# The latent attention sections of a two-block transformer: where filler work stands between the jobs

## The reference

```python
h = x * (1.0 + scale[:, None]) + shift[:, None]
hc = cx * (1.0 + scale_c) + shift_c
(a_q, a_i, a_ff, a_fb, b_q, b_k, b_v, c_q, c_k, c_v, d_q, d_k, d_v, g_lat) = jnp.split(h @ w_in, SPLIT_AT, axis=-1)
... # the same fourteen parts of hc @ w_in for the context
y_a, yc_a = hgrn2_mixer(a_q, a_i, a_ff, a_fb, a_qc, ..., ctx_out)       # gated linear recurrence
y_b = merge_heads(global_gqa(qB, [kB, kBc], [vB, vBc]))                 # attention over latent and context keys
y_c = merge_heads(diff_attention(qC, [kC, kCc], [vC, vCc], lam, ...))   # differential attention
y_d = merge_heads(window_gqa_latent(qD, kD, vD, kDc, vDc, wn_sink))     # window attention
y = jnp.concatenate([y_a, y_b, y_c, y_d], axis=-1) * jax.nn.silu(g_lat)
x_new = layer_norm(alpha * x + gate[:, None] * (y @ w_out), ln_g, ln_b)
```

## Time and profile before

| | |
|---|---|
| median of 3 executions | 1631.5 us |
| profiled execution | 1634.02 us, span 1631.9 us |
| PE busy | 1477.5 us (91%) |
| DVE, ACT, POOL busy | 544.0, 476.0, 146.0 us |
| section two0, from its attention's first logits to its layer norm's end | about 992 to 1323 us |
| section two1 | about 1323 to 1632 us |

### The profile page before, as it was taken

The page is one execution under the profiler, slowest core; times in us unless marked ns, Lnnn a source line. Parts: engine busy times, 40 slices in busy tenths (PEclk is TensorE's granted clock), DMA queues, the critical chain, the costliest instruction groups (busy, mean ns, idle before and its releaser), DMA issues. The chain is left out here.

```text
span 1631.9 us, 20313 instructions
## 1 busy us (share of the span) xinstructions
PE 1477.5 (91%) x8186; PEld 1194.2 (73%) x8186; DVE 544.0 (33%) x1273; ACT 476.0 (29%) x791; POOL 146.0 (9%) x191
## 2 busy tenths in 40 slices
PE   5999999999899999999999999988977866788874
PEld 3887887888788788888888886766765755566654
DVE  1352122112153223233453213556343113563321
ACT  2122333110212333341322424233453014334322
POOL 0111100000010200001110000222000001330000
PEclk8999999999999999999999999998987978898977
DMA  8544344554354444443333343522421312111100
GB/s 360 212 173 163 137 178 155 184 203 181 137 203 177 155 157 177 152 149 129 117 118 128 110 149 147 214 104 104 155 72 70 129 52 103 52 52 52 52 1 26
DMA packets 30765, 219.87 MB, mean 135 GB/s; under 512 B 3792, under 2 KB 3920, under 8 KB 4304
## 3 DMA queue, kind: packets, MB, share of 16 engines
q1 hardware_dynamic: 30672, 218.57, 36.4%
HBM read 217.51 MB, written 1.05 MB: 134 GB/s over the span
## 5 line engine op out<-in xcount | busy, mean ns | idle before, releaser
L811 PE MATMUL event<-u,ring 128*128 128x256 f32 x3200 | 728.6, 388 | 24.2 <-DVE u L1606 13.2
L811 PEld LDWEIGHTS event<-u,ring 128*128 128x128 f32 x3200 | 616.3, 194 | 128.8 <-issue 43.1
L804 PE MATMUL event<-ring,u 128*128 128x256 f32 (+1 forms) x704 | 153.2, 377 | 0.0
L804 PEld LDWEIGHTS event<-ring,u 128*128 128x128 f32 x704 | 130.4, 194 | 22.2 <-issue 5.4
L985 PE MATMUL event<-region,ring 128*128 128x256 f32 x544 | 119.1, 379 | 2.9 <-DVE region L1626 2.9
L1153 ACT ACTIVATE region<-event 128x512 f32<-128x512 f32 x72 | 43.0, 597 | 255.0 <-PE event L811 254.6
L985 PEld LDWEIGHTS event<-region,ring 128*128 128x128 f32 x544 | 102.8, 190 | 17.9 <-issue 4.2
L896 PE MATMUL logits<-region 64*128 64x256 f32 (+4 forms) x320 | 68.5, 531 | 49.4 <-ACT PT L1198 32.3
L1812 POOL TENSOR_TENSOR raw<-raw,tables 128x512 f32<-128x512 f32 (+1 forms) x28 | 34.0, 1215 | 862.5 <-DVE turned L1469 546.2
L1182 ACT ACTIVATE S<-logits,stat 128x512 f32<-128x512 f32 (+2 forms) x160 | 83.9, 536 | 88.9 <-DVE stat L1504 82.4
L960 PE MATMUL event<-region,ring 128*128 128x256 f32 x384 | 84.4, 380 | 0.0
(11 more groups left out here) (200 smaller groups left out, 1315.8 us busy)
## 6 DMA issues: line engine op xcount, KB each, us to landing
ring<-in_w SPq DMA_DIRECT2D x202, 1024.0 KB, 4.8
tables<-in_two SPq DMA_DIRECT2D x1, 1600.0 KB, 9.5
x<-in_x SPq DMA_DIRECT2D x1, 1024.0 KB, 15.5
x<-in_ctx SPq DMA_DIRECT2D x1, 1024.0 KB, 6.6
out<-x SPq DMA_DIRECT2D x1, 1024.0 KB, 3.9
tables<-in_one SPq DMA_DIRECT2D x1, 832.0 KB, 8.5
tables<-in_late SPq DMA_DIRECT2D x1, 512.0 KB, 5.7
consts<-in_common SPq DMA_DIRECT2D x1, 320.0 KB, 3.2
```

Of the source, the lines that this page charges most:

```text
L804: ins = mm(bank[:, t * 256:t * 256 + width], mem.u[:, q, k, t * P:(t + 1) * P], wt[:, k * 256:k * 256 + width], start=k == 0, stop=k == KB ...
L811: ins = mm(bank[:, j * 256:(j + 1) * 256], wt[:, k * 256 + j * P:k * 256 + j * P + P], mem.u[:, q, k, :], start=k == 0, stop=k == KB - 1)
```

## The change

Three edits. First, the wait quoted above stays only where one of jobs n-2, n-1, n is of kind C (stick-breaking attention of the first block, which uses the tile `turns` for logits too). Second, the filler of `two0` is laid out anew: from about one and a half blocks per job in the first half to one block per job through to job 14; the modulation groups are spread likewise, and the context's `kk` and `vv` leave the attention. Third, the context's `vv`, `fv` and `kk` stand at the end of `two0`, between and behind `mean` and `var` (the context's `fk` stays behind the last job). With `kk` so late, `sq gk1` and `norm gk1`, the norm of the context's keys, go from `two0` to the start of `two1`, and the first logits there wait for it.

```diff
--- before.py
+++ after.py
@@ -260,29 +260,28 @@
-    for h, items in ((0, [proj("hq")]), (1, [proj("hi")]), (2, [proj("nq")]), (3, [("rot", "nq", 0)]), (4, [out(1)]), (5, [out(2)]),
-                     (6, [out(3)]), (7, [("mean", 1)]), (8, [proj("fk"), ("var", 1)]), (9, [proj("fq"), ("rot", "fk", 0)]),
-                     (10, [proj("fv"), ("rot", "fq", 0)]), (11, [("mod", "v1"), ("feed", 1, "v1")]),
...
-                     (26, [proj("vv", 1)]), (28, [("gate", 0, 0)])):
+    for h, items in ((0, [proj("hq")]), (2, [proj("nq")]), (3, [("rot", "nq", 0)]), (4, [out(1)]), (6, [proj("hi")]), (7, [out(2)]),
+                     (9, [proj("fk")]), (10, [out(3)]), (11, [("mean", 1), ("rot", "fk", 0)]), (12, [proj("fq"), ("var", 1)]),
+                     (13, [("rot", "fq", 0)]), (14, [proj("fv"), ("mod", "v1"), ("feed", 1, "v1")]), (15, [proj("ff", 1)]),
...
-    for h, items in ((18, [("decay", 1)]), (19, [("prep", 1, "khat")]), (21, [("khatT", 1)]), (23, [("state", 1)])):
+    for h, items in ((20, [("decay", 1)]), (22, [("prep", 1, "khat")]), (24, [("khatT", 1)]), (26, [("state", 1)])):
         fill[h] += items
-    for g, h in enumerate((1, 3, 5, 7, 13, 16)):
+    for g, h in enumerate((1, 5, 8, 11, 16, 20)):
         fill[h] += group("v1", g)
         fill[h + 1].append(("ada", g, "v1"))
     s += weave(len(jobs), fill)
     s += [("sq", "f0"), proj("fk", 1), ("norm", "f0"), ("gate", 0, 1)] + [("out", i, (0,)) for i in range(4)]
-    return s + [proj("fv", 1), ("mean", 0), ("var", 0), ("feed", 0, "v1")]
+    return s + [("mean", 0), proj("vv", 1), ("var", 0), proj("fv", 1), proj("kk", 1), ("feed", 0, "v1")]
@@ script_two1
-         ("rot", "gk", 0), proj("fb"), ("norm", "gq0"), proj("hq"), ("rot", "gq", 0), ("decay", 0)]
+         ("rot", "gk", 0), proj("fb"), ("norm", "gq0"), ("sq", "gk1"), proj("hq"), ("rot", "gq", 0), ("norm", "gk1"), ("decay", 0)]
@@ tensor, item "logits"
-                eng.wait_ge(sems["turns_copied"], w.at("turns_copied", n - 1))
+                if "C" in [j.kind for j in sec.jobs[max(n - 2, 0):n + 1]]:
+                    eng.wait_ge(sems["turns_copied"], w.at("turns_copied", n - 1))
...
+                        if n == 0 and sec.name == "two1":
+                            eng.wait_ge(sems["normed"], w.at("normed", sec.index(("sq", "gk1")) + 1))
```

More of the change, by code:

```diff
@@ L262, in script_two0 @@
     fill = [[] for _ in range(2 * len(jobs))]
-    for h, items in ((0, [proj("hq")]), (1, [proj("hi")]), (2, [proj("nq")]), (3, [("rot", "nq", 0)]), (4, [out(1)]), (5, [out(2)]),
-                     (6, [out(3)]), (7, [("mean", 1)]), (8, [proj("fk"), ("var", 1)]), (9, [proj("fq"), ("rot", "fk", 0)]),
-                     (10, [proj("fv"), ("rot", "fq", 0)]), (11, [("mod", "v1"), ("feed", 1, "v1")]),
-                     (12, [proj("g", 0, 0)]), (14, [proj("ff", 1)]), (15, [proj("fb", 1)]), (17, [proj("kk", 1)]),
-                     (18, [proj("hi", 1), ("sq", "gk1")]), (19, [("norm", "gk1")]), (20, [proj("g", 0, 1)]), (22, [proj("g", 0, 2)]), (24, [proj("g", 0, 3)]),
-                     (26, [proj("vv", 1)]), (28, [("gate", 0, 0)])):
+    for h, items in ((0, [proj("hq")]), (2, [proj("nq")]), (3, [("rot", "nq", 0)]), (4, [out(1)]), (6, [proj("hi")]), (7, [out(2)]),
+                     (9, [proj("fk")]), (10, [out(3)]), (11, [("mean", 1), ("rot", "fk", 0)]), (12, [proj("fq"), ("var", 1)]),
+                     (13, [("rot", "fq", 0)]), (14, [proj("fv"), ("mod", "v1"), ("feed", 1, "v1")]), (15, [proj("ff", 1)]),
+                     (17, [proj("fb", 1)]), (19, [proj("g", 0, 0)]), (21, [proj("hi", 1)]), (23, [proj("g", 0, 1)]),
+                     (25, [proj("g", 0, 2)]), (27, [proj("g", 0, 3)]), (28, [("gate", 0, 0)])):
         fill[h] += items
```

## The result

The changed kernel takes 1593.88 us (median of 4 executions, 1592.23 to 1595.55), the kernel before 1630.87 us beside it: a ratio of 0.9774, 95% interval 0.9757 to 0.9791. A second comparison gave 1590.6 against 1630.02 us, ratio 0.9756 (0.9743 to 0.9770). The forecast was 1594.5 us. The profiled execution took 1595.55 us with a span of 1593.5; the span is 38.4 us shorter than before, of which 0.7 us lies ahead of `two0`'s first logits, where the second and third edit change nothing (that stretch took between 987.2 and 992.2 us in all the profiles here).

A forecast was written before the change was run, and what follows sets the result against it. PE's lost time, idle or at the lower clock, is all the change can win: 22.7 + 11.5 - 1 - 2.7 + 6.4 = 36.9 us off the 1631.5 us median gives 1594.6, predicted as 1594.5 us, range 1588 to 1600.

The forecast's parts named there:

- Term 1: End of `two0`: blocks placed between and behind `mean` and `var` cover waits of 4.92 and 13.20 us; gain 22.7 us.
- Terms 2 and 3: `two0`'s attention: less idle time and slow work in the middle, gain 11.5 us; last jobs and `gate` cost 1 us.
- (b): `two0`'s attention: `rot fq` waits for the bank of level 64, whose DVE copy stands behind `var`'s scaling; 4.2 us.
- (c): `two0`'s attention: level 128 waits for the bank of `ada`, which DVE reaches 6.0 us after `var`'s scaling; 4.0 us.
- (d): `two0`'s attention: `ff` waits for `feed`, which DVE starts after the copy of `fv`; 2.8 us, plus 1.5 us slow.
- Term 4: Start of `two1`: the norm of the context's keys ahead of `decay` makes job 1's logits 2.7 us later.
- Term 5: `two1`'s attention: with the wait for the copy removed, logits start when the exponentials are in; gain 6.4 us.
- R4: Slower: the recurrence's chain over POOL, ACT and DVE bounds all nine levels of `two0`; 1660 us, chance 0.03.
- R1: Even filler hides nothing more in `two0`'s attention: new waits are longer, the clock is lost twice; 1606 us, chance 0.20.
- R3: The copies only change places: the wait returns in `mix` or a level, no gain in `two1`; 1601 us, chance 0.10.
- R2: Long waits in `two0`'s attention shrink more: (b) to (d) half as long, no slow work behind; 1584 us, chance 0.12.

The follow-up runs named there:

- fillers_ahead: The changed kernel with the context's `vv`, `fv` and `kk` all ahead of `mean` and `var`: 1614.75 us.
- norm_early: The changed kernel with the norm of the context's keys moved ahead of block `ff` in `two1`: 1588.95 us, run again unchanged 1590.02 us.
- only_wait: The kernel before with the first edit alone, so logits no longer wait for the copy, layout as before: 1615.45 us.
- var_first: The changed kernel with the context's `var` ahead of block `fq` in `two0`: 1583.64 us, run again unchanged 1580.78 us.

## Why the prediction was right

Every idle time was right to within 1 us per stretch. Two of the terms were off by 4 to 6 us in opposite directions, both in the same part, the slow work, and that the sum is so close is luck.

**Term 1**, predicted 22.7. Between the end of the output blocks and the first block of `two1` that follows the stretch, 44.7 us became 36.4 with two blocks (13.8 us) more: 22.1. fillers_ahead, which undoes nothing but the order, costs 20.9. The margin of 0.6 us that I gave `feed` held, since `feed` ended at 1296.01 and the block ahead of the first one of `two1` at 1296.71; the weights' 0.48 us I missed.

**Terms 2 and 3**, predicted 11.5 less 1, measured 6.1: from the first logits to the last output block 296.3 us before, 276.4 after and 13.8 of blocks moved. The idle part of term 2 was right: 22.3 to 15.8 us (predicted 14.9), and the heirs came where they were named, 1.89, 4.16, 3.51 and 2.76 us for 1.9, 4.2, 4.0 and 2.8. `decay`'s was 2.04 instead of 0.5, `gate`'s 7.89 instead of 7.3. The step that failed is "the slow work ... near 9" falling to 4.5. PE's busy time, less the blocks, did not fall (196.0 against 209.3 - 13.8 = 195.5). I had charged 3 us behind (b) and (c), which is what the rows show, and 1.5 behind (d), where `ff` took 3 us too much, and nothing behind the short waits. Yet behind 1.89 us `mva` took 3.54 us, in other executions 1.93, and behind `decay`'s 2.04 us logits and block took 1.44 and 8.50 us, 1.6 too much. The second profile of norm_early shows that 4.5 us of this are not fixed by the program. Whether the kernel before has such a faster form too I can't tell from its one profile. The lower bound of the gain, -8 us, was added up wrongly: 31 less 14.9 + 11 + 9 is -4; the forecast does not use it.

**Term 4**, predicted +2.7, measured +2.6: from the first block of `two1` behind that stretch to the second logits 52.25 us before (1333.13 to 1385.38) and 54.83 after. DVE and ACT after:

```profile
1346.64 0.48 DVE L1655 SCALAR_TENSOR_TENSOR region<-region,par,rs 128x256 f32<-128x256 f32 x1 [3.90 <-ACT rs L1228]
1347.16 1.76 DVE L1667 TENSOR_SCALAR region<-region,small 128x256 f32<-128x256 f32 x4
```

```profile
1343.05 1.28 ACT L1226 ACT_TABLE_LOAD   x1
1344.34 0.47 ACT L1226 ACTIVATE rs<-event,eps 128x256 f32<-128x256 f32 x1
1344.83 1.28 ACT L1228 ACT_TABLE_LOAD   x1
1346.13 0.42 ACT L1228 ACTIVATE rs<-rs 128x256 f32<-128x256 f32 x1
```

The first four steps took 1.76 us, since POOL had ended at 1345.5, and norm_early put them back beside POOL and to 3.47. One by one these are 0.41, 1.23, 1.30 and 0.41 us there, as in the kernel before, and each of the two long ones began inside an instruction of POOL and ended 0.15 us behind it. The Trainium skill, SBUF — State Buffer, "Who interferes with whom", calls the shared port pair an exclusive lock; both runs agree. The loads took 1.28 us and the next step began 0.01 to 0.02 us later; the drain of 1.38 us that ScalarE: Activation LUTs of the Trainium skill, "What ACT_TABLE_LOAD costs", adds to each switch is not there.

**Term 5**, predicted 6.4, measured 12.2 (185.5 to 173.3 us). The idle part was right, 5.9 in the profile after and 6.2 in only_wait. The term was mis-sized by the clock: PE's busy time fell by 6.4 us and by 7.7 in only_wait; in the ten profiles without the wait other than the two of the kernel after the stretch took 170.7 to 172.5 us, so that 12.2 is the low end. I had priced a wait by its length alone, although showed logits at 2.08 us behind 3.44 and at 1.72 behind 3.46, where 1.13 is their time at the full clock.

**Rivals.** R4 (the recurrence's chain) falls, and so does R1 (nothing in the middle) as far as the idle time goes, which fell by 6.5 us; its other half, that the clock is lost again, is what happened. R3 is half true in `two0`, where only_wait shows the copy's wait return as 2.92 us on ACT and 4.87 on DVE, and false in `two1`. R2 falls: (b) to (d) are 10.4 us together, near the 11.0 reckoned.

The sum, 36.9 against 37.0 by the executions and 37.8 by the stretches above (22.1 + 6.1 - 2.6 + 12.2), owes its closeness to two errors that cancel: 4.4 us too much in the attention of `two0`, 5.8 too little in `two1`. The second comparison measured 39.4 us, so that even the 0.1 us of distance is an accident of the first.

## What to carry to other kernels

On an in-order engine follow every wait to its last cause and look for the heir of each; idle time found like that came out within 1 us in each of the stretches. Price a wait twice, by its length and by the work behind it at the lower clock, but with a range, since the second part differs between executions of one program. When single gains are to be added, add the idle times, measure the common reference again, since its error enters every one of them, look in each trace whether the gain lies where the edit is, and compare the sum with one run of all of them together; and put long blocks exactly where a chain over other engines is open, since the same blocks ahead of the chain left all 18.1 us of its waits.

## What the runs showed of the hardware

- The clock behind waits of 2 to 4 us is not a function of the program: in two profiles of norm_early the mva pair behind the same 1.89 us took 1.93 and 3.56 us and the block behind 2.76 us 8.53 and 10.05, with a granted clock of 0.94 and 0.92 over the stretch; in var_first the pair took 3.38 and 1.93.
- Behind each of the three waits of 2.8 us in `two1` the logits ran at the full clock (1.13 us) in ten of twelve profiles, and the block behind the first took 7.17 us; in the two of the kernel after the second logits took 2.08 and that block 8.86. Logits at the full clock do not mean that nothing was lost: the block behind the second wait took 8.84 to 9.18 us in all twelve.
- A VectorE step (TENSOR_SCALAR, 128x256 f32) of 0.41 us that began while GpSimd's TENSOR_TENSOR ran took 1.23 or 1.30 us and ended 0.15 us behind it, in the kernel before and in norm_early.
- At the first block of `two1` the ring of weights was 0.48 us late in the kernel after (0.56 in the second profile), while the kernel before waits for weights only in its first 25 us. Of the two profiles of var_first one shows 0.19 us there and the other nothing, and norm_early shows nothing in either, so this wait is not fixed by the program either; its cause was not looked for.
